# An expert stage's gate and up weights laid out in runs of eight rows, and the tokens' columns in the same order

## The reference

```python
x = layer_norm(alpha * x + g1 * y, ln1_g[i], ln1_b[i])
x = layer_norm(alpha * x + g2 * hier_moe(modulate(x, sh2, sc2), *moe_w), ln2_g[i], ln2_b[i])

def modulate(u, shift, scale):
    return normalize(u) * (1 + scale) + shift

# in hier_moe: each token goes to 2 of 32 experts; for each expert e and its tokens xb
(jax.nn.silu(xb @ w_gate[e]) * (xb @ w_up[e])) @ w_down[e]
```

## Time and profile before

| | us |
|---|---|
| median of 3 runs | 1722.27 (1721.08 to 1724.59) |
| the profiled execution | 1716.82 |
| its span, first to last instruction | 1714.9 |
| TensorE busy, in the span | 1509.1 |
| VectorE busy | 927.6 |
| ScalarE busy | 692.2 |
| GpSimd busy | 210.0 |

### The profile page before, as it was taken

The page is one execution under the profiler, slowest core; times in us unless marked ns, Lnnn a source line. Parts: engine busy times, 40 slices in busy tenths (PEclk is TensorE's granted clock), DMA queues, the critical chain, the costliest instruction groups (busy, mean ns, idle before and its releaser), DMA issues. The chain is left out here.

```text
span 1714.9 us, 47244 instructions
## 1 busy us (share of the span) xinstructions
PE 1509.1 (88%) x19436; PEld 1103.2 (64%) x19436; DVE 927.6 (54%) x1854; ACT 692.2 (40%) x1585; POOL 210.0 (12%) x274
## 2 busy tenths in 40 slices
PE   5799998999968899878999888956999999997768
PEld 3588885779857788855666667744555555554433
DVE  5798752331125565559899856774153353354416
ACT  5544431112234455535677734422141443333321
POOL 0000101000043544404000000000000000000014
PEclk8899999999988999998999999977999999999889
DMA  9312315550133343230020044319768889999876
GB/s 363 119 62 85 115 60 205 174 174 30 62 122 110 110 124 120 89 126 27 19 74 14 13 145 160 123 53 358 283 236 308 323 325 394 397 396 396 335 241 249
DMA packets 154396, 305.32 MB, mean 178 GB/s; under 512 B 10719, under 2 KB 57391, under 8 KB 150835
## 3 DMA queue, kind: packets, MB, share of 16 engines
q1 hardware_dynamic: 132306, 244.94, 39.6%
q0 software_dynamic: 10336, 46.67, 7.7%
q10 hardware_dynamic: 11520, 10.49, 2.0%
HBM read 256.40 MB, written 45.66 MB: 176 GB/s over the span
## 5 line engine op out<-in xcount | busy, mean ns | idle before, releaser
L2730 PE MATMUL psum<-now_hidden,i_xm 128*32 128x256 f32 x4992 | 291.9, 387 | 18.9 <-DVE now_hidden L2831 15.7
L2730 PEld LDWEIGHTS psum<-now_hidden,i_xm 128*32 128x32 f32 x4992 | 160.5, 111 | 142.6 <-issue 32.0
L2742 PE MATMUL psum<-now_down,i_hT 128*32 128x256 f32 x2464 | 148.3, 381 | 5.8 <-ACT now_down L2793 5.8
L2847 DVE TENSOR_TENSOR i_h<-i_silu,psum 128x128 f32<-128x128 f32 x78 | 22.2, 285 | 219.7 <-ACT i_silu L2786 219.7
L2776 ACT ACTIVATE i_xm<-psum,modT 128x128 f32<-128x128 f32 x163 | 63.4, 458 | 160.1 <-issue 133.4
L2831 DVE COPY now_hidden<-raw_hidden 128x1024 f32 x168 | 104.3, 693 | 33.1 <-DMA raw_hidden<-in_w_up 24.0
L2742 PEld LDWEIGHTS psum<-now_down,i_hT 128*32 128x32 f32 x2464 | 81.5, 110 | 59.0 <-ACT now_down L2793 9.0
L123 PE MATMUL psum<-hT_head,wm_head 128*128 128x512 f32 (+1 forms) x256 | 96.9, 378 | 11.2 <-DVE hT_rest L414 6.9
L1913 PE MATMUL psum<-dkT,f_qT 64*128 64x512 f32 (+1 forms) x384 | 89.0, 571 | 17.3 <-ACT f_E L1963 14.8
L1963 ACT ACTIVATE f_E<-psum,f_mx 128x1280 f32<-128x1280 f32 (+2 forms) x96 | 92.9, 972 | 17.9 <-DVE f_mx L2024 17.0
L123 PE MATMUL psum<-hT_head,wm_rest 128*128 128x512 f32 (+1 forms) x256 | 95.2, 372 | 0.0
(11 more groups left out here) (377 smaller groups left out, 3034.5 us busy)
## 6 DMA issues: line engine op xcount, KB each, us to landing
raw_hidden<-in_w_gate SPq DMA_DIRECT2D x22, 2048.0 KB, 20.0
raw_hidden<-in_w_up SPq DMA_DIRECT2D x22, 2048.0 KB, 24.6
raw_down<-in_w_down SPq DMA_DIRECT2D x22, 2048.0 KB, 21.3
wa_late<-in_w_ada POOLq DMA_DIRECT2D x16, 1024.0 KB, 5.4
yb<-i_y ACTq DMA_DIRECT2D x80, 128.0 KB, 7.6
wa<-in_w_ada SPq DMA_DIRECT2D x8, 1024.0 KB, 13.7
wt<-in_w_in SPq DMA_DIRECT2D x4, 2048.0 KB, 8.6
wm<-in_w_in SPq DMA_DIRECT2D x12, 512.0 KB, 3.9
```

What stands on the lines that cost most here:

```text
L2730: last = nc.tensor.matmul(by_blocks(hidden_bank(s)[j * SUB:(j + 1) * SUB, :]), xm[u][:, k, s * SUB:(s + 1) * SUB], columns_of(now["hidden" ...
L2742: last = nc.tensor.matmul(down_bank(s)[j * SUB:(j + 1) * SUB, :], hT[s % 2][:, k * SUB:(k + 1) * SUB], now["down"][:, k, j * WIDE:(j + 1) ...
```

## The change

Partition p now holds the eight neighbouring rows 8p to 8p + 7 of `w_gate[e]` and `w_up[e]`, at steps k = 0 to 7, 16 KB in one piece of DRAM and one piece of its SBUF row. Down weights stay as they were. The eight transposes take columns k, k + 8, k + 16, ... of the gathered tokens, so that the turned tile k has channel 8p + k on partition p. Scale and shift for `shape` come from a new tile `run_mod`, loaded from DRAM in the same order: for that the rows 3 and 4 of `mod_rows` are stored in `delta_inputs`. 1 is added to the scale by VectorE, and ScalarE waits for that (`mod_ready`).

```diff
-            def store_rows(g, chunks, to):
+            def store_rows(g, chunks, to, done):
...
-            store_rows(0, (0, 1), 2)
+            store_rows(0, (0, 1), 2, rows_stored[0])
+            store_rows(0, (2, 3), 3, expert_rows_stored)
...
-            store_rows(1, (2, 3), 5)
+            store_rows(1, (0, 1), 4, expert_rows_stored)
+            store_rows(1, (2, 3), 5, rows_stored[1])
...
+    def load_runs(n, dst, done):
+        src = m.dram[f"w_{n}"].rearrange("e (a p r) n -> e p a (r n)", p=P, r=RUN)
+        sp.dma_start(dst.rearrange("p (a r) n -> p a (r n)", r=RUN), one(src, e).rearrange("e p a n -> (e p) a n")).then_inc(done, 16)
...
-        load("gate", raw["hidden"][:, h, 0, :, :], loaded["hidden"][h])
-        load("up", raw["hidden"][:, h, 1, :, :], loaded["hidden"][h])
+        load_runs("gate", raw["hidden"][:, h, 0, :, :], loaded["hidden"][h])
+        load_runs("up", raw["hidden"][:, h, 1, :, :], loaded["hidden"][h])
...
+    run_mod = m.keep["run_mod"] = m.sb("run_mod", [P, 2, KD])
...
+        for w in range(2):
+            sp.dma_start(run_mod[:, w, :].rearrange("p (a r) -> p a r", r=RUN),
+                         d["mod_rows"][3 + w].rearrange("(a p r) -> p a r", p=P, r=RUN)).then_inc(gate_loaded, 16)
         sp.wait_ge(planned, 1)
...
+    def run_columns(x, k):
+
+        return x[:, :].rearrange("t (a p r) -> t a r p", p=P, r=RUN)[:, k // RUN, k % RUN, :]
...
-                last = nc.tensor.transpose(m.bank(k // 4)[:, k % 4 * P:(k % 4 + 1) * P], xg[u][:, k * P:(k + 1) * P], ident)
+                last = nc.tensor.transpose(m.bank(k // 4)[:, k % 4 * P:(k % 4 + 1) * P], run_columns(xg[u], k), ident)
...
-                                            scale=modT[:, 4 * KD + k, 0:1], bias=modT[:, 3 * KD + k, 0:1])
+                                            scale=run_mod[:, 1, k:k + 1], bias=run_mod[:, 0, k:k + 1])
...
         act.wait_ge(routed, 1)
         act.sem_inc(loads["down"][1], 16)
+        act.wait_ge(mod_ready, 1)
...
-        dve.wait_ge(gate_loaded, 16 * SUBS)
+        dve.wait_ge(gate_loaded, 16 * (SUBS + 2))
+        nc.vector.tensor_scalar(run_mod[:, 1, :], run_mod[:, 1, :], 1.0, None, ALU.add).then_inc(mod_ready, 1)
```

More of the change, by code:

```diff
@@ L45 @@
 SLOTS = 3
+RUN = 8
 HOT = 229312 - 4 * 4 * KD * DE
@@ L742, in token_inputs @@
     bias_loaded = [m.sem(f"ada_bias_loaded{g}") for g in range(2)]
+    expert_rows_stored = m.sem("ada_expert_rows_stored")
     rows_stored, scaled = [m.sem(f"ada_rows_stored{g}") for g in range(2)], m.sem("ada_scaled")
@@ L786, in store_rows @@
                     sp.dma_start(d["mod_rows"][to:to + 1, n * PIECE:(n + 1) * PIECE], parts[g][32 * c:32 * c + 1, :]
-                                 ).then_inc(rows_stored[g], 16)
+                                 ).then_inc(done, 16)
             def load_bias(g):
@@ L822, in _ @@
             sp.wait_ge(stored, 16 * 2 * TL)
+            sp.wait_ge(expert_rows_stored, 64)
         @block.gpsimd
@@ L2601, in experts @@
     xm = [m.sb(f"i_xm{u}", [P, KD, P]) for u in U2]
-    rep_g = m.keep["rep_g"]
+    rep_g, run_mod, mod_ready = m.keep["rep_g"], m.keep["run_mod"], m.sem("i_mod_ready")
     routed, gate_loaded, first_kept = m.keep["routed"], m.keep["gate_loaded"], m.sem("i_first_kept")
```

## The result

The changed kernel takes 1709.23 us (median of 6 runs, 1704.62 to 1713.12), the kernel before beside it 1722.47 us (6 runs, 1720.26 to 1724.59). The ratio is 0.9934, with a 95% interval of 0.9913 to 0.9956: 13.2 us faster (7.6 to 15.0).

The account below looks back on a forecast made before the run. Expert stage bound by TensorE before about 1450 us, then by DMA order. Longer pieces -9.0, turns before the restart +9.1, last turn +0.8: +0.9 on 1722.3 gives 1723.2 us; own range 1719 to 1727, whole range 1711 to 1731.

Parts of the forecast that it names:

- The bound of each half of the stage: Expert stage: TensorE's time counts before about 1450 us; from there to 1624.65 us the order of DMAs sets the end.
- The price of longer pieces: Gate and up loads in 16 KB instead of 2 KB pieces: 1.0 us less full DMA time for each expert.
- 11 x 0.83 = 9.1 us later: Eleven token turns before 1452.41 us, each 0.83 us longer from the stepped read, delay the DMA restart by 9.1 us.
- rival 1: Token turns: the stepped read costs TensorE nothing, so -9.0 us, 1713.3 us; chance 0.27.
- Rival 2: Expert stage's start: first gather lands 4.3 us later behind 16 KB pieces; with the step's cost +5.2, 1727.5 us; chance 0.14.
- Rival 3: Gate and up loads: longer pieces move no faster, so the turns' cost stands alone, +9.9, 1732.2 us; chance 0.13.
- the loads pace the turn with nothing to spare: Token turn on TensorE: its eight weight loads take 0.86 of 1.09 us, so a longer load lengthens the turn.
- 9 x 1.0 = 9.0 us: Nine gate and up pairs issued after 1452.41 us, each 1.0 us faster, bring the last up 9.0 us earlier.
- the down at 1452.41 us: Sync queue in the expert stage: taken as the restart of a dry queue, with DMA gains before it lost.
- The down forecast for 1461.5 us: Sync queue: the DMA restart at 1452.41 us was to come near 1461.5 us after the change.

Follow-up runs that it names:

- e9: Kernel before, with TensorE doing every turn of token rows twice: 1731.91 us, ratio 1.0071.
- e10: Kernel before, with only the first half of each expert's down weights loaded and copied twice: 1695.18 us, ratio 0.9853.
- e4: Changed kernel with runs of two neighbouring rows instead of eight, 4 KB pieces: 1716.21 us, ratio 0.9965.
- e5: Changed kernel with runs of four neighbouring rows instead of eight, 8 KB pieces: 1712.62 us, ratio 0.9948.
- e1: Kernel before with only the transposes changed, reading token columns eight floats apart: 1722.43 us, ratio 1.0007.
- e2: Changed kernel with the transposes put back on packed columns: 1710.01 us, ratio 0.9935.
- e3: Changed kernel with eight neighbouring rows kept, but gate and up interleaved by row in SBUF, so 2 KB pieces: 1724.20 us, ratio 1.0013.
- e7: Changed kernel with the next expert's gate and up issued ahead of this expert's down: 1720.92 us, ratio 1.0001 to the kernel before.
- e8: Kernel before with the next expert's gate and up issued ahead of this expert's down: 1734.31 us, ratio 1.0078.
- e6: Kernel before with only the small additions: four row stores, two run_mod loads, VectorE's addition, ScalarE's wait: 1723.65 us, ratio 1.0003.
- e11: Changed kernel with only the first half of each expert's down weights loaded and copied twice: 1697.72 us, ratio 0.9857 to the kernel before.
- e12: Changed kernel with down weights in 16 KB pieces too, VectorE's copies reading in steps of four elements: 1768.36 us, ratio 1.0269 to the kernel before.

## Why the prediction was wrong

**What held.** The bound of each half of the stage: TensorE's time is paid ahead of the last restart of the loads (e9), and behind it the transfers' time is (e10). The price of longer pieces, 1.0 us an expert, as a mean. The gate and up pieces of an expert went from 2048 to 256. The window from the down after the gap to the last up's copy, before and then after (each starts at that issue and ends at the earlier trace rows's last copy and the one that answers to it):

```profile
1398.80:1622.10 223.30, 205.05 (x3468) 118.99 (x3464) 90.84 (x200) 86.71 (x160) 8.52 (x9) 0.97 1.03 390
```

```profile
1410.35:1620.98 210.63, 201.77 (x3460) 118.64 (x3460) 90.85 (x199) 86.44 (x160) 8.51 (x9) 0.98 1.00 407
```

The same work in 12.7 us less, at 407 in place of 390 GB/s. Twelve pairs of gate and up are issued in it: 1.06 us each. Over 16 DMA engines 12 x 1792 pieces fewer are 1344 on each, an estimated 9 ns a piece beside its bytes.

That is a mean of two unlike parts. In the last four experts, where the DMA engines stay full, the pieces give 6.3 us, 1.6 us an expert or an estimated 14 ns a piece (10 to 13 by e4 and e5):

```profile
1548.23:1622.10 73.87, 61.32 (x984) 34.68 (x984) 29.11 (x63) 25.31 (x46) 2.83 (x3) 0.92 1.03 390
```

```profile
1553.42:1588.19 34.77, 33.15 (x569) 19.75 (x560) 14.52 (x32) 15.77 (x26) 1.76 (x2) 1.00 1.02 419
1588.19:1620.98 32.79, 29.85 (x480) 16.93 (x484) 14.40 (x31) 13.43 (x25) 1.07 (x2) 0.90 1.02 418
```

In the eight before them it is 6.4 us, 0.8 us an expert; there the faster transfers dip while the queue waits for a slot (241 GB/s from 1462 to 1466 us, 326 from 1530 to 1534). So the predicted 1.0 us is met as a mean; for a queue that is always full it was too small.

The Trainium skill, "DMA: Bandwidth & Descriptors", section "Why small descriptors are slow (HBM only)", has the sign right, but its some 3 cycles a packet would have given an estimated 0.4 us an expert, as the prediction worked out; the measurement decides.

**The step that failed: "11 x 0.83 = 9.1 us later".** The turn was to take 1.9 us and takes 1.16. Price per turn: 0.07 us (e1, e2). From the second turn's start to the eleventh's 205.24 us pass before and 205.76 after, +0.5 us for nine turns in place of +7.5. I had priced TensorE's load by the nearest row that has a step, a VectorE sum, another engine's. All of my chance but rival 1's 0.27 stood on this, since rivals 2 and 3 count the step's cost as well; rival 1 had the right mechanism. The trace speaks against the reason that I gave for it, too: "the loads pace the turn with nothing to spare" came from 0.86 us of busy time for eight loads of 140 ns each, 1.12 us in sum. Their records overlap, so a longer load need not lengthen the turn by as much. That row of single durations was there to be asked for.

The Trainium skill, "SBUF — State Buffer", section "Door 1: The DMA port swizzle", would have a read slow once fewer than two of its elements lie in a 16-byte line. The runs don't show such a threshold for TensorE's loads: 140 ns packed, 209 with two elements to a line (e4), 210 with one (e5), 193 with a step of two lines.

**A second error, in the size of the first term ("9 x 1.0 = 9.0 us"): nine experts counted where twelve count.** I took the down at 1452.41 us for the restart of a queue that had run dry, that is, one with no weights under way. The up issued ahead of it had not landed. Its line and landing time, in the trace of before:

```profile
L2333 SPq DMA_DIRECT2D raw_hidden<-in_w_up x1: 7442/7442/7442, 1431.1 to 1431.1; - x1
...
DMA to landing us min/median/max: 24.4/24.4/24.4
```

1431.11 + 24.4 = 1455.5, 3.1 us behind the down's issue. The last true gap ends with the down at 1398.80 us:

```profile
1367.23 10.10 SPq L2333 DMA_DIRECT2D raw_hidden<-in_w_up  x1
1398.80 0.37 SPq L2333 DMA_DIRECT2D raw_down<-in_w_down  x1
```

The up lands 25.3 us after its issue, at 1392.5, so for 6.3 us no weights were under way (the stretch reads 129 GB/s and a DMA share of 0.43, from gathers and stores). After the change that gap is 9.7 us (an up issued at 1366.66 lands 34.0 us later, the down goes at 1410.35): here the faster transfers do lose what they gain, as I had said of 1452.41. At the later place they lose little: the up issued at 1429.12 lands at 1463.8 and the next down goes at 1462.48, so even the faster queue does not run empty, though it dips to 241 GB/s from 1462 to 1466 us.

**The sum, put right**: -12.7 (twelve pairs) + 0.6 (ten turns of 0.06, the 0.5 us for nine, ahead of 1398.80) + 0.07 (the last turn) = -12.0 us; measured -13.2 (-7.6 to -15.0). That the two lie so close is partly luck. From the first hidden product to the end the changed kernel's profiled execution is 13.2 us shorter too (522.1 in place of 535.3), but two terms of it stand outside this sum. One is +1.8 us at the very start, where the granted clock stayed at its lower level (0.50) for some 4 us into the first hidden product in place of 1:

```profile
1179.65 4.14 PE L2730 MATMUL psum<-now_hidden,i_xm 128*32 128x256 f32 x64 [0.63 <-ACT i_xm L2776]
```

```profile
1188.82 5.92 PE L2747 MATMUL psum<-now_hidden,i_xm 128*32 128x256 f32 x64 [0.70 <-ACT i_xm L2793]
```

The other is -2.9 us from the last hidden product's start to the end. Neither follows the pieces: with 2 KB ones the first product takes 5.4 us in e3 and 5.3 in e10; the end is taken up below.

The down forecast for 1461.5 us went at 1462.48 us. That is luck and proves nothing: the stage began 9.2 us later in this execution, and the turns ahead of that down cost next to nothing.

**The rivals.** Rival 1 (nothing for the step) holds; its 1713.3 us is short by the three experts. Rival 2 (first gather later) is false: from its issue to the first turn 8.3 us pass, before 8.7; gathers do land later in the median, 9.5 us instead of 8.6, but as they are issued two quads ahead, no wait of TensorE shows it.

```profile
1177.90 1.05 POOL L2430 DMA_INDIRECT i_x<-xn,tok  x1 [382.08 <-DVE tok L2537]
...
1186.18 1.94 PE L2739 MATMUL psum<-mask,i_x 128*128 128x128 f32 x8 [8.27 <-issue]
```

Rival 3 (longer pieces no faster) is false by e2, e4 and e5.

**What stays open.** From the last hidden product to `combine`'s first VectorE operation the changed kernel is 2.6 us shorter in the profiled executions. It is not the change's: that stretch, 17.8 us before and 15.2 after, is 15.2 to 15.7 us in e2, e3, e7, e8, e9 and e10 and 17.1 to 17.9 in e1, e4, e5, e6 and e11, so both lengths come with 2 KB pieces and with longer ones. What sets it, and what sets when the clock rises in the first hidden product, was not tried. Nor is the price of a piece by its length settled: the intervals of the times are too wide, and the lengths in the traces are of one execution for each kernel.

## What to carry to other kernels

Before one takes an issue for the restart of a dry queue, add the landing time of the DMA before it to that one's issue: if the sum lies behind, the queue never ran dry, and every transfer back to the last true gap counts. Price a changed operand read by a row of the same engine, and where there is none, give "nothing" the weight that it has; where the durations of single instructions sum to more than their group's busy time, they overlap, and one of them can grow with little to be seen of it. Where transfers end last, fewer and longer pieces pay by their count, but not if another engine must then read with a step on every byte.

## What the runs showed of the hardware that was not expected

- Longer pieces of a load from DRAM still pay between 2 and 16 KB: with full DMA engines 390, 405, 415 and 419 GB/s at 2, 4, 8 and 16 KB for gate and up (down in 4 KB throughout). Each piece saved is worth an estimated 10 to 14 ns on its DMA engine there, 9 ns over the whole stretch of twelve experts. What lies next to a piece in DRAM makes no difference (e3: 388 GB/s).
- TensorE's weight load of 128 x 128 float32 takes 140 ns packed and 193 to 210 ns with a step of 8, 16 or 32 bytes; eight in a row lose 0.11 us for the 32-byte step and 0.17 us for the others (0.86 us, then 0.97, and 1.03 to 1.04).
- VectorE's copy of 1024 float32 elements goes from 693 to 1134 ns with a step of 16 bytes in its source (e12).
- The issue of a load on the sync queue took up to 11.7 us with 2 KB pieces and mostly 0.4 us, at most 6.4, with 16 KB ones; no run shows a gain from that by itself.
